# Narrow attention heads: values as the weights and probabilities as the stream, in a two-block transformer kernel

## The reference, cut to what matters

```
# block 1, in each of 2 layers: 8 query heads, 2 groups of keys and values, three branches
p_cmp = softmax(q kc^T, blocks that have ended)      # 31 compressed keys
p_slc = softmax(q ks^T, causal)                      # 512 keys: top 16 of 8 blocks, so all
p_win = softmax(q kw^T, causal, window 512)          # 512 keys
o = gate0 * p_cmp @ vc + gate1 * p_slc @ vs + gate2 * p_win @ vw      # 64 channels
# block 2: 4 differential heads (values of 128 channels) and 8 grouped heads (values of 64)
o1, o2 = attend(q1, k1, v), attend(q2, k2, v)        # 768 keys, v has 128 channels ("wide")
og = attend(gq, gk, gv)                              # 768 keys, v has 64 channels ("narrow")
```

## Time and profile before

| | |
|---|---|
| median of three executions | 4940.77 us (4940.35 to 4947.4) |
| profiled execution, its own time | 4943.09 us |
| its span, first to last instruction | 4941.2 us |
| mean granted clock of TensorE over the span | 0.781 |
| PE busy, records | 3716.7 us (75%), 15836 |
| DVE, ACT, POOL busy | 46%, 18%, 17% |

### The profile page before, as it was taken

The page is one execution under the profiler, slowest core; times in us unless marked ns, Lnnn a source line. Parts: engine busy times, 40 slices in busy tenths (PEclk is TensorE's granted clock), DMA queues, the critical chain, the costliest instruction groups (busy, mean ns, idle before and its releaser), DMA issues. The chain is left out here.

```text
span 4941.2 us, 45285 instructions
## 1 busy us (share of the span) xinstructions
PE 3716.7 (75%) x15836; PEld 2755.9 (56%) x15836; DVE 2277.7 (46%) x4496; ACT 885.9 (18%) x1350; POOL 833.0 (17%) x610
## 2 busy tenths in 40 slices
PE   6589448987859636989765388872135999999998
PEld 5357326875637524877155066752135777777764
DVE  2122533322122343332122343136889788877765
ACT  2122113322212112321022042221000000000001
POOL 0010000000000000000000021000047555555553
PEclk9755559998965557999887585696555999999998
DMA  3310012321230002321622121021057899888896
GB/s 107 114 35 1 18 52 77 98 96 50 104 106 1 18 18 71 95 91 70 221 84 99 56 62 27 26 92 46 16 179 254 290 318 318 315 320 319 321 400 250
DMA packets 206348, 646.48 MB, mean 131 GB/s; under 512 B 32690, under 2 KB 45778, under 8 KB 201940
## 3 DMA queue, kind: packets, MB, share of 16 engines
q1 hardware_dynamic: 128692, 368.98, 22.5%
q0 software_dynamic: 73728, 268.47, 15.1%
q10 hardware_dynamic: 3744, 6.69, 0.4%
HBM read 610.22 MB, written 32.24 MB: 130 GB/s over the span
## 5 line engine op out<-in xcount | busy, mean ns | idle before, releaser
L109 PE MATMUL psum<-sbuf 128*128 128x512 f32 (+1 forms) x1744 | 689.0, 395 | 245.9 <-DVE sbuf L265 114.9
L110 PE MATMUL psum<-sbuf 128*128 128x512 f32 (+1 forms) x1744 | 684.9, 393 | 0.0
L111 PE MATMUL psum<-sbuf 128*128 128x512 f32 (+1 forms) x1744 | 683.6, 392 | 0.0
L109 PEld LDWEIGHTS psum<-sbuf 128*128 128x128 f32 x1744 | 334.7, 192 | 326.4 <-DVE sbuf L265 117.3
L1711 POOL DMA_INDIRECT sbuf<-peer_u,sbuf x256 | 382.3, 1493 | 792.7 <-issue 611.5
L1747 PE MATMUL psum<-sbuf 128*128 128x512 f32 x1024 | 469.8, 602 | 0.0
L1738 PE MATMUL psum<-sbuf 128*128 128x256 f32 x2048 | 465.5, 381 | 0.0
L1738 PEld LDWEIGHTS psum<-sbuf 128*128 128x128 f32 x2048 | 390.7, 191 | 107.3 <-issue 60.3
L933 POOL TENSOR_TENSOR sbuf<-sbuf 64x768 fp32r<-64x768 f32 (+2 forms) x22 | 29.2, 1325 | 2451.5 <-ACT sbuf L894 2451.5
L1711 POOL DMA_INDIRECT sbuf<-peer_v,sbuf x256 | 352.9, 1379 | 275.6 <-DVE sbuf L1836 201.7
L111 PEld LDWEIGHTS psum<-sbuf 128*128 128x128 f32 x1744 | 334.4, 192 | 69.4
(11 more groups left out here) (261 smaller groups left out, 4273.4 us busy)
## 6 DMA issues: line engine op xcount, KB each, us to landing
sbuf<-peer_ut SPq DMA_DIRECT2D x128, 512.0 KB, 8.5
sbuf<-peer_v SPq DMA_DIRECT2D x128, 512.0 KB, 6.5
sbuf<-w_ffn SPq DMA_DIRECT2D x88, 512.0 KB, 3.5
sbuf<-w_mod SPq DMA_DIRECT2D x12, 2048.0 KB, 7.7
sbuf<-w_fm SPq DMA_DIRECT2D x46, 512.0 KB, 3.6
sbuf<-w_down SPq DMA_DIRECT2D x16, 1408.0 KB, 6.0
sbuf<-w_out SPq DMA_DIRECT2D x24, 512.0 KB, 3.5
sbuf<-cw SPq DMA_DIRECT2D x4, 2048.0 KB, 10.1
```

The costliest lines, as they stand in the source:

```text
L109: nc.tensor.matmul(acc, w_high(k), x_high(k), start=(k == 0), stop=False)
L110: nc.tensor.matmul(acc, w_high(k), x_low(k), start=False, stop=False)
L111: mm = nc.tensor.matmul(acc, w_low(k), x_high(k), start=False, stop=(k == kt - 1))
```

## The change

For narrow calls `values` is replaced by `sums` and `turn_sums`. `sums(i, j)` takes the values of key block j with their column of ones as the weights (65 columns) and streams the probabilities of all queries that see it (512 for full and small items; 512, 384, 256, 128 for causal ones). The result is channel-major, 65 rows by 512 queries, accumulated over j. All of an item's `sums` are dealt out between the shifts of the next item, one for each key block; causal items no longer do part of theirs in their own loop. ACT copies the result to SBUF (`copy_sums`), and TensorE transposes it with four products into bank 2 of `summed` (`turn_sums`) at the end of the loop two items later, from where DVE finishes it. So `finish` runs two items late where it ran one item late. Wide calls are as before.

```diff
+        if not wide:
+            sums_sb = sb([W, 2, S])
...
+            def sums(i, j):
+
+                x = items[i]
+                if j == 0:
+                    if x.first_v:
+                        pe.wait_ge(v_landed[x.v], 16)
+                    if i >= 2:
+                        pe.wait_ge(sums_copied, i - 1)
+                pe.wait_ge(exp_read, block0[i] + j + 1)
+                mm = nc.tensor.matmul(summed[0:W, i % 2, x.q0[j]:S], v[0:x.kw[j], x.v, j, :],
+                                      prob[0:x.kw[j], i % 2, j, x.q0[j]:S], start=(j == 0), stop=(j == x.kt - 1),
+                                      skip_group_check=True)
+                if j == x.kt - 1:
+                    mm.then_inc(pv_done, 1)
+
+            def turn_sums(i):
+                pe.wait_ge(sums_copied, i + 1)
+                if i:
+                    pe.wait_ge(taken, i)
+                for t in range(ST):
+                    mm = nc.tensor.transpose(summed[:, 2, t * W:(t + 1) * W], sums_sb[:, i % 2, t * P:(t + 1) * P],
+                                             C.ident[0:W, 0:W])
+                mm.then_inc(sums_turned, 1)
...
-                late = [] if i == 0 or items[i - 1].kind == "causal" else list(range(ST))
-                if i and items[i - 1].kind == "causal":
-                    late = [ST - 1]
+                late = [] if i == 0 else list(range(ST if wide else items[i - 1].kt))
...
                     for t in late[:-(-len(late) // left)]:
-                        values(i - 1, t)
+                        if wide:
+                            values(i - 1, t)
+                        else:
+                            sums(i - 1, t)
                     late = late[-(-len(late) // left):]
-                    if x.kind == "causal" and j:
-                        values(i, j - 1)
-            for t in range(ST - 1 if items[-1].kind == "causal" else 0, ST):
-                values(N - 1, t)
+                if not wide and i >= 2:
+                    turn_sums(i - 2)
+            for t in range(ST if wide else items[-1].kt):
+                if wide:
+                    values(N - 1, t)
+                else:
+                    sums(N - 1, t)
+            if not wide:
+                turn_sums(N - 2)
+                turn_sums(N - 1)
...
-                if u == HALVES - 1:
+                if not wide:
+                    dve.wait_ge(sums_turned, i + 1)
+                elif u == HALVES - 1:
...
-                got = summed[:, half % 3, 0:NT * W].rearrange("p (t d) -> p t d", d=W)
+                got = summed[:, half % 3 if wide else 2, 0:NT * W].rearrange("p (t d) -> p t d", d=W)
...
-                if i:
+                if wide and i:
                     for u in range(HALVES):
                         finish(i - 1, u)
+                if not wide and i >= 2:
+                    finish(i - 2, 0)
...
+            def copy_sums(i):
+                act.wait_ge(pv_done, i + 1)
+                if i >= 2:
+                    act.wait_ge(sums_turned, i - 1)
+                nc.scalar.activation(sums_sb[:, i % 2, :], summed[0:W, i % 2, :], ACT.Copy).then_inc(sums_copied, 1)
...
                         if i + 1 < N:
                             placed(i + 1)
+                        if not wide and i >= 2:
+                            copy_sums(i - 2)
```

More of the change, by code:

```diff
@@ L631, in attention @@
          exp_read, pv_done, pv_half, ones_set, floored, inverted, factored, taken, added, top_made, gain_landed,
-         squared, rooted, scaled) = [
+         squared, rooted, scaled, sums_copied, sums_turned) = [
             sem.one(x) for x in (
@@ L635, in attention @@
                 "row_placed", "shifted_made", "exp_read", "pv_done", "pv_half", "ones_set", "floored", "inverted",
-                "factored", "taken", "added", "top_made", "gain_landed", "squared", "rooted", "scaled")]
+                "factored", "taken", "added", "top_made", "gain_landed", "squared", "rooted", "scaled", "sums_copied", "sums_turned")]
         block = ctx.enter_context(nc.Block())
@@ L862, in _ @@
                     maxima(i + LEAD)
-                if i:
+                if wide and i:
                     for u in range(HALVES):
                         finish(i - 1, u)
+                if not wide and i >= 2:
+                    finish(i - 2, 0)
                 if wide and i >= 3 and i % 2:
                     square((i - 3) // 2)
+            if not wide:
+                finish(N - 2, 0)
             for u in range(HALVES):
@@ L918, in _ @@
                             placed(i + 1)
+                        if not wide and i >= 2:
+                            copy_sums(i - 2)
                         if i + LEAD + 1 < N:
                             heighten(i + LEAD + 1)
+            if not wide:
+                copy_sums(N - 2)
+                copy_sums(N - 1)
             if wide:
```

## The result

The changed kernel takes 4752.34 us (median of four, 4747.15 to 4759.86) against 4944.09 us before (median of four). The ratio is 0.9612, with a 95% interval of 0.9594 to 0.9631: 192 us faster. The forecast was 4867 us, with 4815 us as the low end. The direction and the mechanism were right, the forecast gain (76 us from 4943) was less than half of what was measured, and the time lies outside the range.

A forecast was written before the change was run, and what follows sets the result against it. TensorE was taken to bound the calls. From 4943 us, two layers at -38.2 us each and the narrow full call at +3 gave 4870, less 2 for the median: 4867 us; range 4815 to 4937 us.

The forecast's parts named there:

- TensorE bounds the calls, everything else is covered: In the calls TensorE is always busy (143.52 of 143.52 us, thirteen causal items); ACT and DVE a quarter or less.
- Part 1: In values turned to sums: at the same clock no difference; full item 10.3 to 10.2 us, causal 4.2 to 4.25.
- Part 2: Four transposes added for each item, all on TensorE's path: 0.95 us at 0.50 and 0.5 us at 1.00.
- Part 4: Granted clock rises to 1.00 in each layer's causal items after 3.5 items; in the narrow full call slightly below even.
- The price at 1.00: Items once at 1.00: causal 6.7 us, 4.3 us less than before; narrow full 12.6 us, 9.5 us less.
- Small items stay at 0.50: Small items of narrow calls keep the clock at 0.50 and take 6.5 us each, against 5.79 before.
- Once up it stays up: Narrow calls: after its rise the clock holds 1.00, as the wide call held it for its item.
- the rival of a swing by the lull of transposes: Clock falls in the lull at each item's end and rises again; half of the 76 us, 4905 us; chance 9%.
- thirteen loops: Thirteen causal loops in each layer: 3.5 items at +1.05 us and 9.5 at -4.3 us, together -37.2 us.
- the end: Each layer's last two loops and tail: -2 us, and turn_back at half its time, -1.7 us.
- my rival of a rise there: Narrow full call rises too, after three items on average: -36 us in place of +3, 4829 us; chance 28%.
- the case with everything up: Causal stretches and narrow full call all rise to 1.00: 4829 us; a rise at once was allowed 14 us more.

The follow-up runs named there:

- x_pad128: The kernel before, with values stored and streamed 128 columns wide in narrow calls in place of 65; 4741.28 us, ratio 0.9592.
- x_late: x_pad128 with small items streaming 65 columns and full items' tiles of values dealt out in steps 2 to 5, not 0 to 3; 4736.45 us.
- x_turn4: The changed kernel with every set of four transposes of turn_sums done four times over; 4823.0 us, one run.
- x_rawonly: The kernel before with raw over 128 rows in place of 64, values still streaming 65 columns; 4821.96 us, one run.
- x_raw128: x_late with raw contracting over 128 rows in place of 64; 4710.5 us, ratio 0.9524.

## Why the prediction was right in kind and short in size

- *TensorE bounds the calls, everything else is covered.* Right: after the change TensorE is busy for 83.50 of 83.50 us at twice the clock, with ACT busy half of the time.
- *Part 1, streaming is worth nothing at one clock.* Right. With either orientation and a full stream a causal item takes about the same, 6.20 us in x_pad128 and 6.32 us with the change, of which 0.22 are transposes. In the full item, where x_late takes 12.15 us and the change 11.9, the new orientation is worth up to 0.5 us at 1.00.
- *Part 2, the transposes.* Mis-sized: 0.44 and 0.22 us a set, not 0.95 and 0.5. I took the pace of `turn_back` over; its transposes have 128 rows and stream 128 columns of identity, the new ones have 65 of each, and come about twice as fast (0.11 us each for 0.213, at 0.50). A small item cost 6.27 us (forecast 6.5), a causal one at 0.50 11.15 (forecast 12.1).
- *Part 4, the clock rises.* Right, and the step that failed is how soon and where: "in the first few causal items ... I take 3.5 items", and for the full call a rise put "slightly below even" and left out of the sum. In the changed kernel the clock rose 2.9 and 3.8 us into the thirteen causal loops, about a third of an item at 0.50, and 18 us into the second full item. In all nine kernels whose `values` or `sums` are full in columns and rows it rose in the first of the thirteen loops of each layer (in x_turn4, the second), and by the second full item (x_turn4: the third). I had judged the mix by its longest full stretch and set the rest aside as weak; x_rawonly shows that the whole mix counts, a full call coming up with its `values` half empty. That the clock would rise at all was put at 87% and rested on few rows; before x_pad128 nothing had shown that the filling of the stream was the cause.
- *The price at 1.00.* Mis-sized: 6.32 us for 6.7, and 11.9 for 12.6. Of this 0.28 us are the transposes.
- *Small items stay at 0.50.* Right.
- *Once up it stays up.* Right for the changed kernel's narrow calls; the rival of a swing by the lull of transposes did not occur. But the wide call, which I cited as holding, does swing: in the kernel before its clock fell at 2922.74, right behind the window of the earlier trace rows, and that item took 14.4 us for 12.8; in the changed kernel it fell three times.

The working, against the rows: thirteen loops -60.0 for -37.2 us. Of the 22.8 missing, 3.2 items fewer at 0.50 make 3.2 x (12.1 - 6.3) = 18.6, the lower price of the other 9.5 items 9.5 x 0.38 = 3.6, and the lower price of the short stretch at 0.50 makes 0.3. The first causal loop -3.3 for -1.6, the small loops +2.9 for +4.3, the end -5.9 for -3.7. That is -66.3 for -38.2, twice. The full call gave -63.7 for +3, and even my rival of a rise there had -36: it priced the loops (-43.2 measured, from the third `place` to the last) and nothing behind them, where the last two items and `turn_back` gave another 20.5. Together 2 x 28 + 67 = 123 us: 4870 - 123 = 4747, against 4749.5 measured for the profiled execution.

The range had a slip of its own. For a rise at once it allowed 14 us below the case with everything up, 4829 us. By the terms of the sum 3.5 items in each layer at 6.7 for 12.1 us are 2 x 3.5 x 5.4 = 38 us, so the low end should have been some 4790 us; the measured time lies outside that too, by the full call.

## What to carry to other kernels

Where a stretch is bound by TensorE and reads 0.50 although it is busy throughout, look at what each product fills: streamed columns against the 128 of a weight load that sets the pace anyway, and rows. Filling the columns with padding was as good here as turning the product round, and needed one line; 96 columns gave little, so it has to be tried and read from the clock line. Once the clock is up, a wait of TensorE can cost more than twice its length (2.4 us of waiting made items of 5.3 us take up to 10.9); look for what the doubled pace makes late, on POOL's queue as much as on ACT and DVE.

## What the runs showed of the hardware that was not expected

- Padding 65 streamed columns to 128 left the pace of a record at 0.215 us at 0.50 (x_pad128, twelve from 2875.35 to 2877.93) and took the causal item from 11.04 to 6.20 us by the clock. 96 columns did nothing in the loops.
- 64 rows in place of 128, with as many products and columns, kept a fully busy TensorE at 0.50 for 168 us; the item was also 1.8 us longer at that clock.
- Products of 64 rows beside products of 128 cost more than the same columns over 128 rows: making `raw` 128 rows high took 0.87 us off a small item and 1.1 us off a causal one at the same clock.
- A transpose came every 0.11 us with 65 rows and 65 columns of identity (x_turn4) and every 0.21 us with 128 of both, at 0.50.
- What stays open: why the clock fell after five waits of 2.4 us and held through a sixth of the same length in the same call (items of 9.52 and 7.93 us in x_raw128); what makes it fall in some items of the wide call and not in others, with the same wait of 0.5 us in each; whether rows in use act by themselves or through the pace; and how far weight columns matter for the moment of the rise.
